# One core of Trainium2: the order in which a gathered expert layer opens its last stage

## The chip, the core and the metric

The kernel runs on one core of a Trainium2 chip. Its time is the device time of one execution in microseconds (us). Three runs of the kernel before gave 1788.18 us in the median (1787.76 to 1791.38).

## What is computed

Two transformer blocks follow each other on 256 tokens of width 1024, all in float32. Only the end of the second block is touched by the change. It is a layer of retrieved experts:

```python
q = (xn @ wq).reshape(bsz, s, PEER_HEADS, 2, PEER_HALF)          # 8 heads, 2 halves of 128
sub = einsum('bshpd,hpnd->bshpn', q, subkeys)                     # against 128 subkeys each
s_top, i_top = top_k(sub, 16)
cand = s_top[..., 0, :, None] + s_top[..., 1, None, :]            # 16 x 16 candidates
best, pos = top_k(cand, 16)                                       # 16 experts per head
gate = softmax(best)
a = gelu(einsum('td,ted->te', xn, u_tab[expert]))                 # 128 experts per token
h = h + einsum('te,ted->td', gate * a, v_tab[expert])
```

For each token and each of its 8 x 16 = 128 chosen experts one row of `u_tab` and one of `v_tab` (1024 numbers each) are fetched. The kernel stores both tables side by side as `puv`, so that one row is 8 KB.

## The kernel before

The program has one instruction stream for each engine, written by hand; semaphores count the results. Weights of all matrix products come as 128 x 1024 tiles through a `ring` of 8 slots. A tile is split into two parts so that three matmuls per product give float32 accuracy: ScalarE writes the high part (L767), VectorE the low part (L1044), both up to three tiles ahead of TensorE (`AHEAD = 3`, four slots for split tiles), and TensorE runs 24 matmuls on it (L494 to L496). ScalarE then evicts the result (L774).

The last stage is driven by one list, `PEER`, that `peer_order` writes (L206). Each engine walks the same list and carries out its own share of each step, strictly in this order:

- `queries hd`: the two query tiles of a head (tiles 2hd and 2hd+1; 16 in all). ScalarE and VectorE split tiles up to three ahead, TensorE multiplies, ScalarE evicts.
- `route t hd p`: the choice of experts for 128 tokens (block t) and one head, in five parts. Part 0: TensorE's product with the subkeys (L726), evicted by ScalarE. Parts 1 to 3: VectorE's sorting (from L1597, from L1609, from L1626). Part 3 ends with the indices in `idx`, and with an exponential on ScalarE (L1007). Part 4: VectorE's division (L1648).
- `turn_h`: TensorE turns the normalized tokens to the layout that the dot products need (L736), ScalarE evicts four banks.
- `gather t k`: GpSimd starts two indirect DMAs (L1737), one for choice k and one for k+1. A gather brings one row for each of the 128 tokens, 128 x 8 KB = 1.05 MB. There are 256.
- `dot t k`: VectorE multiplies each of the two gathered halves with the tokens and sums (L1665).
- `second t k`: ScalarE applies the gelu (L1019), the gate (L1023), and builds a diagonal matrix for each (L1029). TensorE multiplies it with the other half of the gathered rows and adds up in PSUM: two halves of 512 columns, each recorded as two matmuls, so 4 records for one gather and 8 for a pair (L749).
- `finish t`: once the 128 rows of a block are done, VectorE adds the result (L1674), and SyncE stores it.

A gather needs a free buffer. There are 17. Seven of them are early (`NE`): pieces of activation buffers that nobody reads once the tokens are normalized and turned. Ten are late: the weight `ring`, the slots of the split tiles, and the place of the operands of the query product. They come free when the last query tile has been multiplied:

```python
if before:
    q.wait_ge(*mm.at("row", *before))
elif n >= NE:
    q.wait_ge(s_lo, NW)
    q.wait_ge(*mm.at("wq", 15))
else:
    q.wait_ge(*dv.at("peer", "h", 7))
    q.wait_ge(*mm.at("turn_h", 1, 1))
```

`before` is the gather whose rows the buffer held, so it waits for TensorE's `second` on it. The seventh early buffer takes one gather only; the other 16 go round.

The list of the kernel before is: head 0's queries and its whole choice; the turning; the queries of heads 1 to 7, with the choice of head 1 between them; then 128 pairs (c = 0 to 127). A pair is gather, dot, one part of a later choice, second, as long as parts are left: 14 choices of five parts, so pairs 0 to 69. Below, "pair c" is this unit.

Of the kernel before, what the change touches and what calls it, by code (L numbers as in the profile page):

```python
# [204 lines left out]

def peer_order(early, late):  # L206

    out = [("queries", 0)] + [("route", 0, 0, p) for p in range(5)] + [("turn_h", t, h) for t in range(2) for h in range(2)]
    for hd in range(1, 8):
        out.append(("queries", hd))  # L210
        if hd >= 3:
            out.append(("route", 0, 1, hd - 3))
    work = [("route", t, hd, p) for t in range(2) for hd in range(8) for p in range(5)][10:]
    routed, buf, use = {(0, 0), (0, 1)}, {}, {}

    def more():
        if work:
            out.append(work.pop(0))
            if out[-1][3] == 3:
                routed.add(out[-1][1:3])  # L220

    free = list(range(early + late))
    for g in range(256):
        t, k = divmod(g, 128)
        n = free.pop(0)
        if n != early - 1:
            free.append(n)
        times, before = use.get(n, (0, None))
        buf[t, k] = n, times + 1, before
        use[n] = times + 1, (t, k)  # L230

    for c in range(128):
        t, k0 = divmod(2 * c, 128)
        while (t, k0 // 16) not in routed:
            more()
        out.append(("gather", t, k0))
        out.append(("dot", t, k0))
        if c == 40:
            out.extend([("turn_y", i // 2, i % 2) for i in range(4)])
        more()  # L240
        out.append(("second", t, k0))
        if k0 == 126:
            out.append(("finish", t))
    return out, buf


def program(nc, T, out, dbg=None):
    ctx = ExitStack()
    with ctx:
# [156 lines left out]
        NB = len(gbuf)  # L406
        s_g = [sem(f"row_in{i}") for i in range(NB)]
        PEER, GB = peer_order(NE, NB - NE)


# [1520 lines left out]
```

## Time and profile before

| what | value |
|---|---|
| median of the runs | 1788.18 us |
| the profiled execution | 1791.73 us, span of its instructions 1789.2 us |
| PE, DVE, ACT, POOL busy in the span | 85%, 64%, 34%, 21% |
| granted TensorE clock, mean | 0.926 |
| bytes read from HBM | 430.29 MB, of which the gathers are 268 MB |
| last stage | from about 1068 us to the end |
| chain that ended last | PE 57%, DVE 23%, DMA 12%, ACT 6% |

The profile is of one execution, and its times count from the span's first instruction. PE is TensorE, DVE VectorE, ACT ScalarE, POOL GpSimd. A row of a timeline gives start, length, engine, line, operation, what is written and read, and in brackets how long the engine had been idle and what ended that. Consecutive instructions of one kind are merged as "x8".

### The profile page before, as it was taken

To read this page: it belongs to the slowest core of one execution; us is meant where nothing else is said; L and a number is where in the kernel's file an instruction comes from. 1 tells how busy PE (TensorE), PEld (TensorE's weight loads), DVE (VectorE), ACT (ScalarE), POOL (GpSimd) and SP (SyncE) were. 2 spreads that over 40 slices of the span, in tenths; PEclk is the share of its full clock that TensorE was granted. 3 is DMA by queue.
4 is the path that set the end of the run, shared out by engine and by line. 5 is a ranking of instruction groups with operands and counts; after the bars stand their busy time and mean duration, and the time that the engine had idled before them with its cause. 6 is when DMAs were issued, how large, how long until landed. Compare 5 with 4: busy or idle time off the path is not lost.

```text
span 1789.2 us, 19560 instructions
## 1 busy us (share of the span) xinstructions
PE 1517.9 (85%) x7194; PEld 1108.8 (62%) x7194; DVE 1144.5 (64%) x2246; ACT 611.0 (34%) x1336; POOL 370.3 (21%) x376
## 2 busy tenths in 40 slices
PE   7899999997887799997988677878778777977776
PEld 6788888886764799997977577533333333432222
DVE  6876765556474665556577655887686777544444
ACT  2322222224244444443453244433333333322222
POOL 2000110010000000010000111444344343743430
PEclk8899999997989799997998888989889897999999
DMA  9554774443220255553331355699999998999997
GB/s 379 186 167 136 232 247 162 136 148 116 84 83 23 95 187 181 175 174 106 116 113 51 100 186 224 240 421 421 421 421 402 394 386 337 417 421 421 421 421 321
DMA packets 86189, 432.60 MB, mean 242 GB/s; under 512 B 9616, under 2 KB 13200, under 8 KB 53072
## 3 DMA queue, kind: packets, MB, share of 16 engines
q0 software_dynamic: 45024, 298.08, 41.9%
q1 hardware_dynamic: 41072, 133.30, 22.8%
q8 instruction: 57, 0.93, 0.2%
q14 instruction: 36, 0.29, 0.0%
HBM read 430.29 MB, written 1.05 MB: 241 GB/s over the span
## 4 chain that ended last, share of the span: by engine, by line
PE 57%; DVE 23%; DMA 12%; ACT 6%; issue 2%; POOL 0%; SPq 0%; DVEq 0%; POOLq 0%; ACTq 0%
PE ps L494 14%; PE ps L495 14%; PE ps L496 14%; DMA HF<-in_puv,AB 11%; PE ps L749 11%; DVE WR L1044 2%; DVE work L1102 2%; ACT WR L767 2%; DVE HF L1665 1%; ACT L1019 1%; DVE ring L1665 1%; DMA ring<-in_w_adaT 1%; DVE WF L1665 1%; PE ps L607 1%; DVE HR L1122 1%
## 5 line engine op out<-in xcount | busy, mean ns | idle before, releaser
L494 PE MATMUL ps<-HR,WR 128*128 128x256 f32 (+1 forms) x1336 | 438.6, 328 | 49.5 <-DVE HR L1122 15.4
L1044 DVE TENSOR_TENSOR WR<-ring,WR 128x1024 fp32r<-128x1024 f32 (+2 forms) x245 | 281.9, 1153 | 240.7 <-ACT WR L767 240.4
L495 PE MATMUL ps<-HR,WR 128*128 128x256 f32 (+1 forms) x1336 | 427.9, 320 | 0.0
L496 PE MATMUL ps<-HR,WR 128*128 128x256 f32 (+1 forms) x1336 | 427.1, 320 | 0.0
L767 ACT CAST WR<-ring 128x1024 fp32r<-128x1024 f32 (+2 forms) x245 | 237.2, 972 | 347.7 <-PE ps L496 347.6
L494 PEld LDWEIGHTS ps<-HR,WR 128*128 128x128 f32 x1336 | 265.0, 198 | 74.9 <-issue 39.4
L495 PEld LDWEIGHTS ps<-HR,WR 128*128 128x128 f32 x1336 | 266.2, 199 | 16.0 <-issue 1.2
L496 PEld LDWEIGHTS ps<-HR,WR 128*128 128x128 f32 x1336 | 265.6, 199 | 14.4
L749 PE MATMUL ps<-HF,AB 128*128 128x512 f32 x252 | 130.3, 652 | 41.6 <-ACT AB L1029 41.6
L749 PE MATMUL ps<-ring,AB 128*128 128x512 f32 x256 | 126.8, 639 | 38.8 <-ACT AB L1029 38.8
L749 PE MATMUL ps<-WF,AB 128*128 128x512 f32 x256 | 125.6, 635 | 34.7 <-ACT AB L1029 34.7
L494 PE MATMUL ps<-AR,WR 128*128 128x256 f32 (+1 forms) x416 | 137.5, 330 | 4.8 <-POOL AR L1719 4.8
L495 PE MATMUL ps<-AR,WR 128*128 128x256 f32 (+1 forms) x416 | 137.2, 330 | 0.0
L496 PE MATMUL ps<-AR,WR 128*128 128x256 f32 (+1 forms) x416 | 137.2, 330 | 0.0
L749 PEld LDWEIGHTS ps<-HF,AB 128*128 128x128 f32 x252 | 50.6, 207 | 112.5 <-ACT AB L1029 56.0
L749 PEld LDWEIGHTS ps<-ring,AB 128*128 128x128 f32 x256 | 50.4, 203 | 109.2 <-issue 54.4
L749 PEld LDWEIGHTS ps<-WF,AB 128*128 128x128 f32 x256 | 50.3, 202 | 105.5 <-issue 55.3
L1019 ACT ACTIVATE AB<-AB 128x2 f32<-128x2 f32 x128 | 25.7, 201 | 239.6 <-DVE AB L1665 239.4
L1665 DVE CUSTOM_DVE_ANT_0 WF<-WF,AF 128x1024 f32<-128x1024 f32 x64 | 77.3, 1220 | 38.1 <-DMA WF<-in_puv,AB 38.1
L1665 DVE CUSTOM_DVE_ANT_0 ring<-ring,AF 128x1024 f32<-128x1024 f32 x64 | 77.1, 1220 | 32.7 <-DMA ring<-in_puv,AB 32.7
L1665 DVE CUSTOM_DVE_ANT_0 HF<-HF,AF 128x1024 f32<-128x1024 f32 x63 | 76.5, 1221 | 31.9 <-DMA HF<-in_puv,AB 31.8
L1694 POOL DMA_DIRECT2D AB<-in_w_adaT x56 | 29.8, 532 | 323.7 <-DVE Mr L1055 282.2
(244 smaller groups left out, 2270.7 us busy)
## 6 DMA issues: line engine op xcount, KB each, us to landing
AB<-in_w_adaT POOLq DMA_DIRECT2D x56, 512.0 KB, 4.7
ring<-in_f1i SPq DMA_DIRECT2D x44, 512.0 KB, 4.5
ring<-in_f2i SPq DMA_DIRECT2D x44, 512.0 KB, 3.5
ring<-in_w SPq DMA_DIRECT2D x33, 512.0 KB, 3.6
ring<-in_mi SPq DMA_DIRECT2D x19, 512.0 KB, 3.5
ring<-in_f1o SPq DMA_DIRECT2D x16, 512.0 KB, 4.2
ring<-in_f2o SPq DMA_DIRECT2D x16, 512.0 KB, 3.5
ring<-in_wq SPq DMA_DIRECT2D x16, 512.0 KB, 4.3
```

The lines of the kernel that those rows point to most:

```text
L494: e.matmul(o, l[0], r[0], start=first, stop=False)
L495: e.matmul(o, l[0], r[1], start=False, stop=False)
L496: return e.matmul(o, l[1], r[0], start=False, stop=last)
L607: x = e.matmul(o[o_:o_ + 64, 0:256], vN[:, k, 64 * kv:64 * kv + 64], PT[:, hd % 2, k, :], start=k == 0, stop=k == 3)
L749: x = e.matmul(psum[ab + h][:, :], D[:, nd % 8, :], gbuf[n][:, 1024 + 512 * h:1536 + 512 * h], start=k == 0, stop=k == 127)
L767: e.copy(WS[:, m % NSP, 0, 0:nk * cols], ring[:, (NA + m) % NS, 0:nk * cols]).then_inc(s_hi, 1)
L1019: e.activation(w_, w_, ACT.Gelu_apprx_tanh).then_inc(*ac.to("gelu", t_, k0))
L1044: e.tensor_tensor(WS[:, m % NSP, 1, 0:nk * cols], ring[:, (NA + m) % NS, 0:nk * cols], WS[:, m % NSP, 0, 0:nk * cols].bitcast(F32), ALU.su ...
L1102: e.reciprocal(r, r).then_inc(*dv.to("recip", *key))
L1122: e.scalar_tensor_tensor(out=low, in0=F[:, f, a], scalar=sh[:, s:s + 1], in1=hi.bitcast(F32), op0=ALU.add, op1=ALU.subtract).then_inc(*dv. ...
L1665: e.tensor_tensor_reduce(u_, u_, hN[:, t_, :], 1.0, 0.0, ALU.mult, ALU.add, av[:, t_, k:k + 1]).then_inc(*dv.to("dot", t_, k))
L1694: e.dma_start(AB[:, 3072 + 1024 * s_:4096 + 1024 * s_], T["w_adaT"][i]).then_inc(s_a[s_], 16)
```

## The change

Only `peer_order` changes. The whole difference:

```diff
-    out = [("queries", 0)] + [("route", 0, 0, p) for p in range(5)] + [("turn_h", t, h) for t in range(2) for h in range(2)]
-    for hd in range(1, 8):
-        out.append(("queries", hd))
-        if hd >= 3:
-            out.append(("route", 0, 1, hd - 3))
-    work = [("route", t, hd, p) for t in range(2) for hd in range(8) for p in range(5)][10:]
-    routed, buf, use = {(0, 0), (0, 1)}, {}, {}
+    out = [("queries", 0), ("route", 0, 0, 0)] + [("turn_h", t, h) for t in range(2) for h in range(2)]
+    out += [("route", 0, 0, 1), ("route", 0, 0, 2), ("queries", 1), ("route", 0, 0, 3), ("route", 0, 0, 4), ("queries", 2)]
+    work = [("route", t, hd, p) for t in range(2) for hd in range(8) for p in range(5)][5:]
+    routed, buf, use = {(0, 0)}, {}, {}
...
-    free = list(range(early + late))
+    free = list(range(early))
     for g in range(256):
+        if g == 13:
+            free = list(range(early, early + late)) + free
...
         out.append(("dot", t, k0))
+        if c < 5:
+            out.append(("queries", c + 3))
         if c == 40:
```

The new list is: head 0's queries, the first part of its choice, the turning, the rest of the choice with head 1's queries between its parts, head 2's queries. Then the pairs begin. The queries of heads 3 to 7 stand inside pairs 0 to 4, after the dot products and before the second product. The choice of head 1 fills pairs 0 to 4 too, and every later choice stands five pairs later than before, so parts are left for pairs 0 to 74. Gathers 7 to 12 use six early buffers a second time; gather 13 is the first that takes a late buffer.

The operations and their number stay the same. On ScalarE, the eviction of the turned tokens (`AF<-ps` of 512 columns) moves ahead of the exponential. Before:

```order
L774 COPY AF<-ps2 128x256
L1007 ACT_TABLE_LOAD
L1007 ACTIVATE AB,small<-AF,small 128x16
L774 COPY AF<-ps3 128x512
L774 COPY AF<-ps0 128x512
L774 COPY AF<-ps1 128x512
L774 COPY AF<-ps2 128x512
L767 CAST WR<-ring 128x1024
L774 COPY AB<-ps3 128x256
L767 CAST WR<-ring 128x1024
```

and now (all lines below L206 stand one line lower):

```order
L775 COPY AF<-ps3 128x512
L775 COPY AF<-ps0 128x512
L775 COPY AF<-ps1 128x512
L775 COPY AF<-ps2 128x512
L768 CAST WR<-ring 128x1024
L775 COPY AB<-ps3 128x256
L768 CAST WR<-ring 128x1024
L775 COPY AB<-ps0 128x256
L1008 ACT_TABLE_LOAD
L1008 ACTIVATE AB,small<-AF,small 128x16
L768 CAST WR<-ring 128x1024
L775 COPY AB<-ps1 128x256
```

The four evictions come first now, then a split tile and a query's eviction, twice, and only then the exponential.

The place where head 1's exponential and the first gelus stand, also ScalarE. Before, from the query evictions on:

```order
L774 COPY AB<-ps2 128x256
L774 COPY AB<-ps3 128x256
L1007 ACTIVATE AB,small<-AF,small 128x16
L774 COPY AB<-ps0 128x256
L774 COPY AB<-ps1 128x256
L774 COPY AF<-ps2 128x256
L1019 ACT_TABLE_LOAD
L1019 ACTIVATE AB<-AB 128x2
L1023 ACTIVATE AB<-AB 128x1 x2
```

and now, in pairs 3 and 4:

```order
L768 CAST WR<-ring 128x1024
L775 COPY AB<-ps2 128x256
L775 COPY AB<-ps3 128x256
L1008 ACT_TABLE_LOAD
L1008 ACTIVATE AB,small<-AF,small 128x16
L1020 ACT_TABLE_LOAD
L1020 ACTIVATE AB<-AB 128x2
L1024 ACTIVATE AB<-AB 128x1 x2
L1030 ACTIVATE AB<-kc,AB 128x128 x2
L775 COPY AB<-ps0 128x256
L775 COPY AB<-ps1 128x256
```

The exponential stands between the evictions of tiles 12 and 13 and those of tiles 14 and 15 as before, but now a table load is ahead of it and another behind it, and the first product of pair 3's rows comes ahead of tiles 14 and 15.

GpSimd's gathers with what they wait for. Before:

```order
L1737 DMA AF<-in_puv,AB 128x2048 [waits pe_group,dve_result]
L1737 DMA AF<-in_puv,AB 128x2048
L1737 DMA HF<-in_puv,AB 128x2048 x2
L1737 DMA work<-in_puv,AB 128x2048 x2
L1737 DMA AF<-in_puv,AB 128x2048
L1737 DMA ring<-in_puv,AB 128x2048 [waits pe_group,low_part]
L1737 DMA ring<-in_puv,AB 128x2048 x3
```

and now:

```order
L1738 DMA AF<-in_puv,AB 128x2048 [waits pe_group,dve_result]
L1738 DMA AF<-in_puv,AB 128x2048
L1738 DMA HF<-in_puv,AB 128x2048 x2
L1738 DMA work<-in_puv,AB 128x2048 x2
L1738 DMA AF<-in_puv,AB 128x2048
L1738 DMA AF<-in_puv,AB 128x2048 [waits pe_group] x2
L1738 DMA HF<-in_puv,AB 128x2048 [waits pe_group] x2
L1738 DMA work<-in_puv,AB 128x2048 [waits pe_group] x2
L1738 DMA ring<-in_puv,AB 128x2048 [waits pe_group,low_part]
```

After the first seven, the next ones wait for TensorE's second product on the gather whose buffer they take, where before the eighth waited for the last query tile; that wait now stands at the fourteenth.

## Rows read from the trace of the kernel before

**Rows 1.** Busy time by stretch; last columns: granted clock, DMA share, GB/s
```profile
core 0: us, PE busy (x) PEld busy (x) DVE busy (x) ACT busy (x) POOL busy (x), PEclk, DMA share, GB/s
1200.00:1300.00 100.00, 76.88 (x161) 33.67 (x162) 72.36 (x204) 34.92 (x114) 40.77 (x35) 0.86 1.01 421
1470.00:1520.00 50.00, 33.99 (x63) 14.21 (x62) 36.84 (x92) 17.95 (x61) 17.52 (x15) 0.80 0.90 348
1555.00:1785.00 230.00, 175.46 (x383) 68.84 (x381) 112.08 (x182) 59.05 (x230) 82.60 (x81) 1.00 0.98 407
```
**Rows 2.** Timeline of PE, the stage's opening: start, length, what [idle before]
```profile
1090.14 0.58 PE L494 MATMUL ps<-HR,WR 128*128 128x256 f32 x1 [8.95 <-ACT AF L774]
...
1133.48 0.61 PE L726 MATMUL ps<-XT,AB 128*128 128x128 f32 x4
...
1136.88 5.33 PE L749 MATMUL ps<-AF,AB 128*128 128x512 f32 x8 [2.79 <-ACT AB L1029]
...
1142.05 3.60 PE L749 MATMUL ps<-HF,AB 128*128 128x512 f32 x8
```
**Rows 3.** Timeline of ACT, the same stretch
```profile
1089.22 0.31 ACT L1007 ACTIVATE AB<-AF,small 128x16 f32<-128x16 f32 x1 [8.06 <-DVE small L1644]
...
1089.52 2.02 ACT L774 COPY AF<-ps 128x512 f32<-128x512 f32 x4
...
1095.67 0.37 ACT L774 COPY AB<-ps 128x256 f32<-128x256 f32 x1 [3.18 <-PE ps L496]
...
1133.68 0.37 ACT L774 COPY AB<-ps 128x256 f32<-128x256 f32 x1 [2.51 <-PE ps L496]
...
1135.81 0.20 ACT L1019 ACTIVATE AB<-AB 128x2 f32<-128x2 f32 x1
...
1148.17 0.31 ACT L1007 ACTIVATE AB<-AF,small 128x16 f32<-128x16 f32 x1 [5.49 <-DVE small L1644]
...
1148.59 1.28 ACT L1019 ACT_TABLE_LOAD   x1
...
1149.89 0.20 ACT L1019 ACTIVATE AB<-AB 128x2 f32<-128x2 f32 x1
```
**Rows 4.** Timeline of DVE, the same stretch
```profile
1079.88 0.29 DVE L1597 MAX8 AF<-AF 128x8 f32<-128x128 f32 x1 [1.66 <-ACT AF L774]
...
1083.16 0.42 DVE L1609 TENSOR_TENSOR AF<-AF 128x256 f32<-128x256 f32 x1
...
1086.27 0.18 DVE L1626 CAST AF<-AF 128x32 f32<-128x32 uint32 x1
...
1124.76 1.22 DVE L1044 TENSOR_TENSOR WR<-ring,WR 128x1024 fp32r<-128x1024 f32 x1
...
1129.61 1.22 DVE L1665 CUSTOM_DVE_ANT_0 AF<-AF 128x1024 f32<-128x1024 f32 x1
...
1158.97 0.29 DVE L1597 MAX8 AF<-AF 128x8 f32<-128x128 f32 x1 [0.90 <-ACT AF L774]
```
**Rows 5.** Timeline of POOL: the first and the eighth gather
```profile
1089.40 1.00 POOL L1737 DMA_INDIRECT AF<-in_puv,AB  x1 [26.88 <-DVE small L1644]
...
1134.42 0.94 POOL L1737 DMA_INDIRECT ring<-in_puv,AB  x1 [35.37 <-PE ps L726]
```
**Rows 6.** The gathers' table, seen by its own view
```profile
DMA to landing us min/median/max: 5.3/21.1/34.0
```
**Rows 7.** Timeline of PE over the repeating part
```profile
1157.92 0.61 PE L726 MATMUL ps<-XT,AB 128*128 128x128 f32 x4
...
1175.42 3.78 PE L749 MATMUL ps<-HF,AB 128*128 128x512 f32 x4 [4.95 <-ACT AB L1029]
...
1185.23 0.61 PE L726 MATMUL ps<-XT,AB 128*128 128x128 f32 x4
...
1458.45 0.61 PE L726 MATMUL ps<-XT,AB 128*128 128x128 f32 x4
...
1492.96 0.61 PE L726 MATMUL ps<-XT,AB 128*128 128x128 f32 x4
```
**Rows 8.** The chain that ended last, in order of time
```profile
1510.46 44.05 PE ps L749 x96
```

## The prediction

> **What bounds the kernel now.** I read the busy time by stretch first, then the timelines of the last stage's opening engine by engine, then the chain of waits. All stages up to 1068 us keep their instructions, so only the last one counts.
>
> By stretch [rows 1], the DMA engines are full from 1200 to 1300 us at 421 GB/s. A gather is 128 x 8 KB = 1.05 MB, so it takes 1.05 / 0.421 = 2.49 us, and a pair 4.98. Between 1470 and 1520 us the share falls to 0.90 and 348 GB/s, at the end it is 0.98. So DMA is nearly the bound, but something else holds it back in the middle. The repeating part shows what. The subkey product opens each choice of experts, once in five pairs. It stands at 1157.92 us, then at 1185.23, and eleven choices after the first at 1458.45 [rows 7]: (1458.45 - 1157.92) / 11 = 27.3 us for five pairs, where DMA needs 24.9. TensorE is idle for 4.95 us in each, waiting for the diagonals behind the choice, and then takes 3.78 us for four records [rows 7], against 3.60 for eight elsewhere [rows 2]: that is the clock at 1.2 and not 2.4 GHz. So **the five-pair loop is slower than DMA by 2.4 us**, and after enough loops the 16 buffers are used up and the loop sets when gathers start. When the last choice is over, TensorE runs 96 records, 24 gathers' rows, in 44.05 us without a pause [rows 8]. That is 1.84 us a row against 2.49, so it catches up with DMA, and DMA alone sets the end.
>
> The end is therefore: start of the loops, plus their number times 27.3, plus what DMA still has to bring. The opening counts by when the loop at pair 5 begins, and in two places by when gathers land.
>
> **The opening of before.** TensorE has turned the tokens by 1081.2 us, then stands for 8.95 us until 1090.14 [rows 2], because ScalarE evicts the turned tokens only at 1089.52, behind the exponential of 1089.22 [rows 3]. The next tile runs at the lower clock, 1090.14 to its eviction at 1095.67. From there 13 tiles and a subkey product take 1133.68 - 1095.67 = 38.0 us, 2.88 a tile. The last query tile is done at 1133.48 [rows 2], and GpSimd starts gather 7 at 1134.42 [rows 5]; 0.95 us later.
>
> **The change, step by step.**
>
> *The turning.* The four evictions no longer wait for the choice. TensorE begins head 1 at 1081.2, at the clock that it has. The saving at the first tile is 1095.4 - (1081.2 + 2.88) = 11.3 us.
>
> *The first gather.* Two split tiles (1.15 us each by their spacing, 1.22 in the row [rows 4]) now stand on VectorE between parts 2 and 3. Part 3 began at 1086.27 [rows 4], and now begins at 1088.6. The first gather starts at 1089.40 + 2.3 = 1091.7 [rows 5]. The shortest time to landing is 5.3 us [rows 6], so it lands by 1097.0, the second no sooner than 1099.5, and its dot product (1.22) ends at 1100.7.
>
> *TensorE, heads 1 and 2 and 3.* Six tiles, 17.3 us, to 1098.5, and 0.6 for the subkey product. Then it waits for the first diagonal: from the gelu to the product takes 1136.88 - 1135.81 = 1.07 us [rows 2, 3], so it starts at 1101.8. That is an idle time of 2.7 us, and after 2.79 us before, the first eight records took 5.33 and not 3.60 [rows 2]. I take 5.33: pair 0 ends at 1107.1.
>
> *Pairs 1 and 2.* Two tiles, 5.76. Then the second product waits for ScalarE, which evicts the second tile first: 0.3 us to its start, 0.27 for it, 1.07 from gelu to product, 1.6 together. Then 3.45 for eight records. 10.8 a pair, to 1128.7. VectorE has in each pair two split tiles, two dot products (1.15 each [rows 4]) and one part of a choice (1079.88 to 1083.16 is 3.3, the next 3.1 [rows 4]), 8 us in all, and hides in TensorE's time. The gathers of these pairs are the first seven and land by about 1115.
>
> *Pair 3.* 5.76 to 1134.5, then 0.57 for the eviction, a table load of 1.28, the exponential 0.42 (1148.17 to 1148.59), a load of 1.30 (1148.59 to 1149.89) [rows 3] and 1.07: product at 1139.1, 4.6 us idle, 5.33 for it, to 1144.4. These two loads are new on the path. I charge 1.3 us for each, what the row shows with everything around it. The Trainium skill ("ScalarE: Activation LUTs", What ACT_TABLE_LOAD costs) says that a switch takes about 2.66 us, since 1.38 us of drain come on top of the load. By the page the two would cost 2.8 us more, and the sum below would be +3.9 and not +1.1.
>
> *Pair 4 and the late buffers.* Two tiles to 1150.2. **The last query tile is 16.7 us later than before**, because four pairs of second products (3.45 to 5.33 each) and the waits around them now stand ahead of it. Gather 13 starts at 1151.1 and lands at 1156.4. Before, it was the seventh behind 1134.42: 1139.7 + 6 x 2.49 = 1154.7. So six gathers early and a late wait nearly cancel, and gather 13 is 1.7 us later than before. The early ones, 7 to 12, take buffers whose rows are done by 1128.7, and land before 1136; they hide.
>
> *Pair 5.* Pair 4's second product ends at 1150.2 + 1.6 + 3.45 = 1155.3, and the subkey product follows, 2.6 us before 1157.92. VectorE must first do pair 6's dot products, the second of them on gather 13, until 1157.6. It begins sorting there and not at 1158.97 [rows 4]. **The loops begin 1.3 us earlier**, and at the same pair c = 5.
>
> *One loop more.* Parts of a choice last for pairs up to 74, not 69. The five pairs 70 to 74 take 27.3 and not DMA's 24.9: +2.4 us. The stop between the two blocks of tokens (1458.45 to 1492.96 is 34.5 and not 27.3 us [rows 7]) lies at pair 64 in both, in the same part of a loop, and costs the same.
>
> *Sum.* -1.3 + 2.4 = **+1.1 us** on the profiled execution's 1791.73. The median of the runs lies 3.5 us below that; I add the change to the median, 1788.18 + 1.1 = **1789.3**. Not shown by the trace is whether a start 1.3 us earlier survives 14 loops, each with its fall of the clock. An earlier product does more of its work at the lower clock, so all of it may be lost (0). Or the fall ends sooner in a loop, which saves at most what the slow four records lose, 3.78 - 1.80 = 2.0 us; allowing that twice beside the 1.3 gives -5.3 for the loops. With the +2.4 the bounds are -2.9 and +2.4.
>
> A measurement of this kernel can tell about 0.2%, 3.6 us, from no change.
>
> **Rivals.**
>
> *Faster, the opening runs without waits.* If ScalarE is never behind and the clock stays up, TensorE's work alone is 1081.2 + 14 x 2.88 + 4 x 3.45 = 1135.3: the late gathers start only 2 us later than before, with 13 done. Pair 5 begins at about 1140, 18 us earlier. Gather 13 lands at 1141.6, 13 us before 1154.7, so DMA then is the limit: -13, about 1775. For it speaks that 24 rows run without a pause [rows 8]; against it that ScalarE's order puts an eviction ahead of every gelu, and in pair 3 the two loads. A part of it would be enough to pass 3.6 us. Chance 0.14.
>
> *Slower, the clock falls in every opening pair.* TensorE stops for 1.6 us in each of the pairs 1, 2 and 4. If each stop brings the lower clock, the product behind it takes 5.33 and not 3.60: 3 x 1.7 = 5.2 us. Sorting at pair 5 then begins 3.9 us later than before, and the late gathers, behind pairs 1 and 2, 3.5 us later still. The end is +1.1 + 5.2 = +6.3, 1794.5. It decides from 2.5 us of added delay in the opening. For it speaks how close 2.79 us of idle time comes, against it that the tiles around the stops are dense work. Chance 0.16.
>
> *Slower, a switch of tables costs more than its row.* The two new loads stand ahead of pair 3's product with nothing beside them, so what a switch costs beyond 1.3 us goes to the end twice. It decides from 1.25 us more in each: +1.1 + 2.5. Against it speaks that between the end of the exponential and the gelu lie 1.30 us, and the load fills 1.28 of them [rows 3]; nothing is left for more. With the cost of one such load paid again each time, the end is 1.1 + 2.6 = +3.7, about 1792. Chance 0.04. This is the case that the Trainium skill's figure, above, would make.
>
> *The early gathers do nothing.* If DMA alone set the end, then only the start of gather 13 would count, +1.7 us. That is inside the forecast's band.
>
> **How the numbers follow.** The forecast with its bounds, and the last rival, stay within 3.6 us: 0.66. Faster 0.14, slower 0.16 + 0.04 = 0.20. For 8 in 10 the range has to reach past the bounds -2.9 to +2.4 to about half of each rival: 1783 to 1795.
>
> **What would show it.** Right: no 9-us gap of TensorE after the turning, first gather about 2.3 us later, the last query tile at 1150 with GpSimd's gather 13 one us behind it, the subkey product of pair 5 at about 1155, the following ones 27.3 apart, and one more of them at the end. Idle times of TensorE of about 2.7, 1.6, 1.6, 4.6 and 1.6 us in pairs 0 to 4. Wrong: a last query tile before 1145 or after 1154 us, loops other than 27.3 us, or a DMA share between 1470 and 1520 us that reaches 1.0.

## The result, and the profile after

The changed kernel took 1797.88 us in the median of six runs (1792.85 to 1798.67). The kernel before, in six runs, took 1788.78 us (1787.23 to 1791.89). The ratio is 1.0044, 95% interval 1.0032 to 1.0057: the change made the kernel slower by 0.3 to 0.6%. The forecast was 1789.3 us, no measurable change, and a range up to 1795. It was wrong.

The profiled executions are 1797.77 us against 1791.73, and their spans 1795.8 and 1789.2, so 6.0 to 6.6 us can be followed in the two traces. The interval of the ratio is 5.7 to 10.2 us, and they lie inside it. In both the last stage begins at the same place: head 0's subkey product starts at 1078.42 us now, and at 1078.33 before.

The timeline of TensorE (PE) in the opening, which answers to [rows 2] and [rows 7]. All names below stand one line lower than before.

```profile
1098.39 0.61 PE L727 MATMUL ps<-XT,AB 128*128 128x128 f32 x4
...
1105.64 5.62 PE L750 MATMUL ps<-AF,AB 128*128 128x512 f32 x8 [6.64 <-ACT AB L1030]
...
1118.37 3.70 PE L750 MATMUL ps<-HF,AB 128*128 128x512 f32 x8 [1.37 <-ACT AB L1030]
...
1129.19 3.70 PE L750 MATMUL ps<-work,AB 128*128 128x512 f32 x8 [1.37 <-ACT AB L1030]
...
1143.14 5.40 PE L750 MATMUL ps<-AF,AB 128*128 128x512 f32 x8 [4.50 <-ACT AB L1030]
...
1155.65 1.98 PE L750 MATMUL ps<-AF,AB 128*128 128x512 f32 x4 [1.37 <-ACT AB L1030]
...
1159.19 0.61 PE L727 MATMUL ps<-XT,AB 128*128 128x128 f32 x4
...
1188.54 0.61 PE L727 MATMUL ps<-XT,AB 128*128 128x128 f32 x4
```

The 8.95 us gap at head 1 [rows 2] is gone. In its place TensorE stops five times: 6.64, 1.37, 1.37, 4.50 and 1.37 us ahead of the products of pairs 0 to 4. The first product took 5.62 us for eight records and the fourth 5.40; those in between took 3.70. Pair 5's subkey product is at 1159.19 and not at 1157.92, and pair 10's at 1188.54 and not at 1185.23: 1.3 us late, then 3.3 us late.

POOL, the first two gathers and the fourteenth (before [rows 5]), then VectorE (DVE) with what it waited for:

```profile
1091.64 1.01 POOL L1738 DMA_INDIRECT AF<-in_puv,AB  x1 [29.01 <-DVE small L1645]
...
1092.95 1.94 POOL L1738 DMA_INDIRECT AF<-in_puv,AB  x1 [0.30 <-issue]
...
1155.06 0.94 POOL L1738 DMA_INDIRECT ring<-in_puv,AB  x1 [20.28 <-PE ps L497]
```

```profile
1092.83 2.44 DVE L1045 TENSOR_TENSOR WR<-ring,WR 128x1024 fp32r<-128x1024 f32 x2 [0.51 <-ACT WR L768]
...
1097.37 1.22 DVE L1666 CUSTOM_DVE_ANT_0 AF<-AF 128x1024 f32<-128x1024 f32 x1 [2.10 <-DMA AF<-in_puv,AB]
...
1103.31 1.23 DVE L1666 CUSTOM_DVE_ANT_0 AF<-AF 128x1024 f32<-128x1024 f32 x1 [4.70 <-DMA AF<-in_puv,AB]
...
1160.59 1.23 DVE L1666 CUSTOM_DVE_ANT_0 ring<-ring,AF 128x1024 f32<-128x1024 f32 x1 [15.94 <-DMA ring<-in_puv,AB]
```

The last query tile was done at 1154.1 us, 0.95 us ahead of gather 13, where before it was 1133.48. Gather 1 was used only at 1103.31, 11.7 us after gather 0 was started.

ScalarE (ACT) in pair 3:

```profile
1139.07 1.28 ACT L1008 ACT_TABLE_LOAD   x1
...
1140.36 0.31 ACT L1008 ACTIVATE AB<-AF,small 128x16 f32<-128x16 f32 x1
...
1140.78 1.28 ACT L1020 ACT_TABLE_LOAD   x1
...
1142.07 0.20 ACT L1020 ACTIVATE AB<-AB 128x2 f32<-128x2 f32 x1
```

A load, the exponential, a load, the gelu: 3.0 us, the loads at 1.28 us and their start.

The busy time by stretch, where the last two columns are the share of the DMA engines and GB/s:

```profile
core 0: us, PE busy (x) PEld busy (x) DVE busy (x) ACT busy (x) POOL busy (x), PEclk, DMA share, GB/s
1116.00:1140.00 24.00, 19.90 (x121) 15.47 (x119) 19.50 (x51) 7.94 (x19) 5.62 (x4) 1.00 0.60 223
1140.00:1155.00 15.00, 11.14 (x56) 7.92 (x56) 3.82 (x8) 4.32 (x13) 0.00 (x0) 0.89 0.00 0
1155.00:1160.00 5.00, 4.14 (x12) 2.04 (x12) 0.00 (x0) 1.06 (x5) 3.74 (x4) 1.00 0.68 223
```

For 15 us, from 1140 to 1155, the DMA engines moved nothing at all. Thirteen gathers had come, and the fourteenth waited for a late buffer.

The end of the repeating part, PE, and the piece of the chain of waits behind it (before [rows 7, 8]):

```profile
1461.96 0.61 PE L727 MATMUL ps<-XT,AB 128*128 128x128 f32 x4
...
1496.44 0.61 PE L727 MATMUL ps<-XT,AB 128*128 128x128 f32 x4
...
1523.48 0.61 PE L727 MATMUL ps<-XT,AB 128*128 128x128 f32 x4
```

```profile
1540.98 54.48 PE ps L750 x120
```

The stop between the blocks is 34.5 us as before. One loop more stands behind it, 27.0 us. The run of products without a pause that catches up with DMA begins at 1540.98 and not at 1510.46, and takes 120 records and not 96.

### The profile page after: what moved, and what is told of

Same layout as the page of the kernel before. It is cut to its first block, busy times and chain, and to the rows that moved or that the text cites. A ratio compares the mean times of both kernels' runs of the same rounds, so it can differ in the third digit from the quotient of the medians.

```text
span 1795.8 us, 19544 instructions
## 1 busy us (share of the span) xinstructions
PE 1521.2 (85%) x7194; PEld 1109.4 (62%) x7194; DVE 1144.0 (64%) x2246; ACT 612.7 (34%) x1338; POOL 373.3 (21%) x376
## 4 chain that ended last, share of the span: by engine, by line
PE 57%; DVE 22%; DMA 11%; ACT 6%; issue 2%; POOL 1%; SPq 0%; DVEq 0%; POOLq 0%; ACTq 0%
PE ps L495 14%; PE ps L496 14%; PE ps L497 14%; PE ps L750 12%; DMA ring<-in_puv,AB 10%; DVE WR L1045 2%; DVE work L1103 2%; ACT WR L768 2%; DVE ring L1666 1%; ACT L1020 1%; DVE WF L1666 1%; DVE HF L1666 1%; DMA ring<-in_w_adaT 1%; PE ps L608 1%; DVE HR L1123 1%
## 5 line engine op out<-in xcount | busy, mean ns | idle before, releaser
L750 PE MATMUL ps<-WF,AB 128*128 128x512 f32 x240 | 121.8, 652 | 37.4 <-ACT AB L1030 37.4
L750 PE MATMUL ps<-AF,AB 128*128 128x512 f32 x140 | 73.2, 659 | 31.5 <-ACT AB L1030 31.5
```

The lines of the kernel that those rows point to most:

```text
L750: x = e.matmul(psum[ab + h][:, :], D[:, nd % 8, :], gbuf[n][:, 1024 + 512 * h:1536 + 512 * h], start=k == 0, stop=k == 127)
```

## The experiments

Two theories stood at first. **Theory A:** the turning ahead of the choice is worth what the opening saves. The interleaving (the queries of heads 3 to 7 inside the pairs) then loses more, since four pairs' products, their waits and a loop more stand ahead of or behind the last query tile. **Theory B:** DMA and the clock set the time, so the opening matters little, and early gathers are worth their transfer. All kernels compute the whole reference. The short diffs are against the kernel named; lines of `peer_order` that only carry the bookkeeping along are left out.

The traces are compared by stage, since the place of the stage's start moved between profiles (last section). "Pair 5" and "pair 10" are the starts of these pairs' subkey products behind the stage's first one; "stage" is the span's end less the stage's first subkey product; "rest" is stage less pair 10. All are from the profiled executions, in us. The loops are those that start at pair 5 or later. Each ratio is against executions of before taken together with the kernel's; their medians were 1788.92 us for e1 to e4, 1789.11 for e5 to e7 and 1787.99 for e8 and e9.

| kernel | median | ratio, 95% | pair 5 | pair 10 | loops | rest | stage |
|---|---|---|---|---|---|---|---|
| before | 1788.78 | | 79.6 | 106.9 | 13 | 604.0 | 710.9 |
| the change | 1797.88 | 1.0044 (1.0032 to 1.0057) | 80.8 | 110.1 | 14 | 607.3 | 717.4 |
| e1, turning alone | 1779.05 | 0.9946 (0.9928 to 0.9963) | 71.8 | 97.8 | 13 | 602.6 | 700.4 |
| e2, no interleaving | 1774.48 | 0.9920 (0.9904 to 0.9936) | 67.9 | 94.1 | 13 | 603.0 | 697.1 |
| e3, one loop more | 1793.21 | 1.0020 (1.0010 to 1.0030) | 79.2 | 106.7 | 14 | 607.6 | 714.3 |
| e4, first gather | 1796.85 | 1.0041 (1.0028 to 1.0055) | 80.5 | 108.2 | 14 | 605.6 | 713.8 |
| e5, two heads inside | 1784.03 | 0.9978 (0.9967 to 0.9989) | 76.9 | 104.1 | 13 | 603.2 | 707.3 |
| e6, one loop less | 1780.66 | 0.9960 (0.9947 to 0.9973) | 77.5 | 104.1 | 12 | 599.6 | 703.7 |
| e7, diagonals first | 1785.30 | 0.9976 (0.9966 to 0.9985) | 69.4 | 100.3 | 14 | 607.3 | 707.6 |
| e8, no first stop | 1783.68 | 0.9976 (0.9967 to 0.9985) | 70.1 | 100.0 | 14 | 607.2 | 707.2 |
| e9, e7 and e8 | 1790.77 | 1.0007 (0.9997 to 1.0017) | 72.5 | 103.8 | 14 | 607.8 | 711.6 |

The column "rest" carries the reading of them all. It is 602.6 to 604.0 with 13 loops, 599.6 with 12, and 607.2 to 607.8 with 14 (605.6 in e4). What happens ahead of pair 10 reaches the end in full, within 1.4 us in all kernels but e4, and a loop costs about 3.5 us. How many gathers are early does not show in it: the change, with thirteen, has 607.3, and e3, with seven and as many loops, 607.6.

### e1: the turning alone

```diff
-    out = [("queries", 0)] + [("route", 0, 0, p) for p in range(5)] + [("turn_h", t, h) for t in range(2) for h in range(2)]
+    out = [("queries", 0), ("route", 0, 0, 0)] + [("turn_h", t, h) for t in range(2) for h in range(2)] + [("route", 0, 0, p) for p in range(1, 5)]
```

> The kernel before, with the turning of the tokens alone moved ahead of parts 1 to 4 of the first choice; all queries stay ahead of the pairs and the buffers stay as before. Theory A (the opening's gain is real, and the interleaved queries lose it again): TensorE goes on after 1081 us for three tiles, waits for the next split tile, and has the last query tile about 8 us before 1133.5; the loops follow, so the end is 6 to 9 us below before. Theory B (DMA and clock decide, the opening does not matter): within 2 us of before.

Measured: 1779.05 us, 9.9 below before in the medians, the stage 10.5 us shorter. Theory A's mechanism held, and its 6 to 9 us were a little low. This part of the change alone is a gain of half a per cent.

### e2: no interleaving

Against before; the two lines after `out` are those of the change.

```diff
-    out = [("queries", 0)] + [("route", 0, 0, p) for p in range(5)] + [("turn_h", t, h) for t in range(2) for h in range(2)]
-    for hd in range(1, 8):
+    out = [("queries", 0), ("route", 0, 0, 0)] + [("turn_h", t, h) for t in range(2) for h in range(2)]
+    out += [("route", 0, 0, 1), ("route", 0, 0, 2), ("queries", 1), ("route", 0, 0, 3), ("route", 0, 0, 4), ("queries", 2)]
+    for hd in range(3, 8):
         out.append(("queries", hd))
-        if hd >= 3:
-            out.append(("route", 0, 1, hd - 3))
+        out.append(("route", 0, 1, hd - 3))
```

> The change's opening up to head 2's queries, but heads 3 to 7 and head 1's choice stay ahead of the pairs, and the late buffers follow the first seven as before. Theory A: last query tile at about 1122 us instead of 1154, gather 7 then, loops 10 to 12 us earlier than before and none more than before: end about 10 us below before. If six gathers more in the early buffers were worth what they bring (15 us), this kernel would lose against the change; theory A has it 18 us ahead of the change.

Measured: 1774.48 us, 14.4 us below before and 23.4 below the change, the fastest kernel of this study; theory A had expected 10 and 18. PE, then POOL's eighth gather; the stage began at 1074.32 here:

```profile
1121.16 5.40 PE L749 MATMUL ps<-AF,AB 128*128 128x512 f32 x8 [2.79 <-ACT AB L1029]
...
1142.22 0.61 PE L726 MATMUL ps<-XT,AB 128*128 128x128 f32 x4
...
1168.39 0.61 PE L726 MATMUL ps<-XT,AB 128*128 128x128 f32 x4
```

```profile
1118.71 0.94 POOL L1737 DMA_INDIRECT ring<-in_puv,AB  x1 [20.38 <-PE ps L726]
```

The last query tile was done 0.95 us ahead of 1118.71, 43.4 us into the stage, against 75.7 in the change (1154.1 - 1078.4). Six gathers fewer were early, and DMA moved nothing between 1112 and 1120 us. Even so, the change, with 13 early gathers, is the slower one by 20.3 us of stage. So the end does not follow DMA's early start. What the six early gathers are worth by themselves this run does not tell, since it changes the place of the queries with them.

### e3: one loop more

Against before: head 1's choice is left out of the opening, and the choices start in pair 0 with head 1.

```diff
         out.append(("queries", hd))
-        if hd >= 3:
-            out.append(("route", 0, 1, hd - 3))
-    work = [("route", t, hd, p) for t in range(2) for hd in range(8) for p in range(5)][10:]
+    work = [("route", t, hd, p) for t in range(2) for hd in range(8) for p in range(5)][5:]
```

> The kernel before with one thing of the change: head 1's choice is made inside pairs 0 to 4, every later one five pairs later, so parts last to pair 74. Last query tile unchanged at 1133.5 us. The loop takes 27.3 us where DMA takes 24.9, so theory A expects +2.4 us, at most +6 if the loops start at another phase of the clock. Rival: the DMA queue absorbs it, 0.

Measured: 1793.21 us, +4.3 in the medians (+1.8 to +5.4 by the interval), +3.4 in the stage. Pairs 5 and 10 stay in place within 0.4 us; the whole of it lies in the rest. So DMA does not absorb a loop, and its price is 3.4 us where I had 2.4.

### e4: the first gather earlier

Against the change:

```diff
-    out += [("route", 0, 0, 1), ("route", 0, 0, 2), ("queries", 1), ("route", 0, 0, 3), ("route", 0, 0, 4), ("queries", 2)]
+    out += [("route", 0, 0, 1), ("route", 0, 0, 2), ("route", 0, 0, 3), ("queries", 1), ("route", 0, 0, 4), ("queries", 2)]
```

> The change, with head 1's queries behind part 3 of the first choice instead of between parts 2 and 3, so the first index is out 2.3 us earlier and the next split tiles 2.9 us later. If the 6.6 us stop of TensorE ahead of pair 0's product (and the slow clock behind it) is what the late first gather costs, pair 0's product starts 2 us earlier and the end is 2 to 4 us below the change; if the landing beside the weight tiles sets it, no difference from the change.

Measured: 1796.85 us, the same as the change within the intervals. In the profile the stage is 3.6 us shorter, but that execution is not a typical one of its kernel (1793.45 us against a median of 1796.85). Pair 0's product:

```profile
1103.76 5.40 PE L750 MATMUL ps<-AF,AB 128*128 128x512 f32 x8 [2.79 <-ACT AB L1030]
```

From the stage's start (1076.53) that is 27.2 us, which is the change's 27.2 (1105.64 - 1078.42) exactly. The first gather went out 2.1 us earlier, but TensorE was behind: head 2's second tile waits for a split tile that now comes later. The stop is shorter by 3.9 us and the product at the same place. The experiment moved the wait and did not take it away, and so does not tell what the late landing costs; e8 takes the long stop away, though not by itself.

### e5: two heads inside

Against e2: heads 3 to 5 stay ahead with all of head 1's choice, heads 6 and 7 go into pairs 0 and 1.

```diff
-    for hd in range(3, 8):
+    for hd in range(3, 6):
         out.append(("queries", hd))
         out.append(("route", 0, 1, hd - 3))
+    out += [("route", 0, 1, 3), ("route", 0, 1, 4)]
...
         out.append(("dot", t, k0))
+        if c < 2:
+            out.append(("queries", c + 6))
```

> Run e2 with the queries of heads 6 and 7 alone inside pairs 0 and 1; head 1's choice stays ahead, loops as many as before, seven early gathers. Theory A (what stands ahead of the last query tile is what counts): the last tile waits for the first gather's landing at about 1103 us and for one pair of rows, so it comes at about 1120 to 1128 (counted with the stage's start at 1078), and the end lies 2 to 10 us above e2. Rival (interleaving costs only by the extra loop and not by the place of the last tile): same as e2 within 2 us.

Measured: 1784.03 us, 9.6 above e2. The stage is 10.2 us longer, pair 10 is 10.0 us later, the rest is equal. So interleaving costs without any loop more, as theory A has it; the rival is out. The last query tile comes 54.7 us into the stage, some 5 us later than theory A had put it.

### e6: one loop less

Against e2:

```diff
+    rr = [("route", 0, h, p) for h in (1, 2) for p in range(5)]
     for hd in range(3, 8):
         out.append(("queries", hd))
-        out.append(("route", 0, 1, hd - 3))
+        out += [rr.pop(0), rr.pop(0)]
```

> Run e2 with head 2's choice ahead of the pairs as well, two parts behind each of heads 3 to 7. One loop less (13), the last query tile unchanged; but VectorE has 10 us more to do before the first dot product, so pair 0 starts about 6 us later. If a loop is worth what e3 showed (3.4 us in the profiles) and the later start is hidden by DMA: 3 us below e2. If the loops' start counts fully: 3 us above e2 or more.

Measured: 1780.66 us, 6.2 above e2. The rest is shorter by 3.4 us, which gives the price of a loop from the other side. But pair 10 comes 10.0 us later, and this start counts in full, as the expectation's second case had it. That VectorE's whole further choice ahead of the first dot product makes it late is the reason given beforehand; no run separates it.

### e7: diagonals first

Against the change, in ScalarE's program alone. It walks a list in which, for pairs 0 to 4, the queries and the part of the choice stand behind the second product's share.

```diff
+            mine, held = [], []
             for s in PEER:
+                if s[0] == "queries" and s[1] >= 3 or held and s[0] == "route":
+                    held.append(s)
+                elif s[0] == "second":
+                    mine += [s] + held
+                    held = []
+                else:
+                    mine.append(s)
+            for s in mine:
```

> The change, with ScalarE alone in another order in pairs 0 to 4: gelu and diagonals come ahead of the two query evictions and of the exponential. The stops of TensorE ahead of the products of pairs 1 to 4 (1.37, 1.37, 4.50, 1.37 us, and the slow clock in pair 3) should go. If they are what the interleaving costs, the last query tile comes 8 to 10 us earlier than in the change and the end lies 7 to 10 us below it. If the second products themselves (four pairs ahead of the last tile, 14 us at full clock) and the first landing are the larger part, it still does not reach run e2: about 1788 against 1774.

Measured: 1785.30 us, 12.6 below the change where 7 to 10 were expected, the stage 9.8 us shorter. PE, the products of pairs 0 to 3:

```profile
1103.16 5.61 PE L750 MATMUL ps<-AF,AB 128*128 128x512 f32 x8 [6.61 <-ACT AB L1039]
...
1114.35 3.60 PE L750 MATMUL ps<-HF,AB 128*128 128x512 f32 x8
...
1123.53 3.60 PE L750 MATMUL ps<-work,AB 128*128 128x512 f32 x8
...
1132.72 3.60 PE L750 MATMUL ps<-AF,AB 128*128 128x512 f32 x8
```

The three later ones start without a stop and at full speed; the first stop of 6.6 us is still there. Pair 5 comes 11.4 us earlier than in the change, pair 10 9.8 us: 1.6 us are lost again in the first loop, 30.9 us long, since gather 13, which pair 6's dot products need, had started only 2.5 us ahead of pair 5's subkey product (1142.85 and 1145.34).

### e8: no first stop

Against the change:

```diff
-    ... ("route", 0, 0, 4), ("queries", 2)]
+    ... ("route", 0, 0, 4), ("queries", 2), ("queries", 3)]
...
-        if c < 5:
-            out.append(("queries", c + 3))
+        if c in (0, 1, 2, 4):
+            out.append(("queries", c + 4 - c // 4))
```

> The change, with head 3's queries ahead of pair 0 and those of heads 4, 5, 6 and 7 inside pairs 0, 1, 2 and 4. As many second products (four pairs) stand ahead of the last query tile as in the change, the same thirteen gathers are early, the same loops follow; but TensorE has two more tiles to do while the first two gathers land. Theory: the stop of 6.64 us ahead of pair 0's product, with the slow clock behind it (5.62 for 3.70 us, and part of the next tile), is the term that was priced too low. Then the last query tile comes 6 to 9 us earlier than the change's 1154 us and the end lies 6 to 9 us below the change, about 1790. Rival (the clock or the landing of gather 13 sets the loops, whatever the first stop): within 2 us of the change.

Measured: 1783.68 us, 14.2 below the change where 6 to 9 were expected, the stage 10.2 us shorter. PE, pairs 0 to 3, with the stage's start at 1074.19:

```profile
1103.32 3.70 PE L750 MATMUL ps<-AF,AB 128*128 128x512 f32 x8 [2.79 <-ACT AB L1030]
...
1114.13 3.70 PE L750 MATMUL ps<-HF,AB 128*128 128x512 f32 x8 [1.37 <-ACT AB L1030]
...
1124.95 3.70 PE L750 MATMUL ps<-work,AB 128*128 128x512 f32 x8 [1.37 <-ACT AB L1030]
...
1129.98 3.70 PE L750 MATMUL ps<-AF,AB 128*128 128x512 f32 x8 [1.32 <-ACT AB L1030]
```

Pair 0's product stops for 2.79 us and takes 3.70 and not 5.62. Pair 3's product follows pair 2's after 1.32 us, where in the change two tiles, the exponential and a fall of the clock lay between. The number of products ahead of the last query tile, the early gathers and the loops are the change's. So of the change's 717.4 us some 10 are stops of TensorE that another order of the same steps avoids. The edit took away more than the first stop, the one of pair 3 too, so it does not split the 10 us between them.

### e9: both

Against the change: the edits of e7 and e8, with `s[1] >= 4` in e7's condition.

> Run e8 with ScalarE's order of run e7 (diagonals ahead of the query evictions and the exponential). If the first stop and the later stops are separate costs, they add: about 15 to 19 us below the change, and of the 23 us between the change and run e2 only the loop more (3.4) and the products ahead of the last tile are left: 1779 to 1783. If DMA's late start takes over (gather 13 lands behind the loops), it stays within 3 us of e7's 1785.

Measured: 1790.77 us, 7.1 above e8 alone, 5.5 above e7, and above both ranges that had been expected (1779 to 1783, or within 3 us of e7). What the two edits save does not add. PE's product of pair 3, and ScalarE ahead of it:

```profile
1136.31 5.76 PE L750 MATMUL ps<-AF,AB 128*128 128x512 f32 x8 [8.48 <-ACT AB L1039]
```

```profile
1133.54 0.31 ACT L1017 ACTIVATE AB<-AF,small 128x16 f32<-128x16 f32 x1 [7.43 <-DVE small L1654]
```

With the diagonals first, ScalarE is early in pair 2 and then stands for 7.43 us at head 1's exponential, which waits for VectorE; the diagonals of pair 3 are behind it. In pair 3 there is no query tile for TensorE to do in that time, so it stops for 8.48 us. The wait that the edit removed came back elsewhere.

## Why the prediction was wrong, by its own steps

- **What bounds the kernel: right.** Loops 27.3 us apart, each dearer than DMA's ten rows; then a run without pause, then DMA. The table's "rest" shows it in all eleven kernels. That gathers' landings count too held for gather 13, which VectorE waited for at pair 6, and for no later one that the table would show.
- **The turning: right in kind.** TensorE went on at once. Pair 0's subkey product came at 1098.39, predicted 1098.5. By e1 this part alone is worth 10 us.
- **The first gather: the step that failed.** I took the second gather's landing at its earliest, 2.49 us behind the shortest landing, 1099.5. Its dot product started at 1103.31, 3.8 us later. A lower bound had been put in as the value. The trace of before already had a better one. Its DMA issues, from issue to landing in us: gathers 0 and 1 of before (issued at 1089.40 and 1090.71), then gather 1 of e7 (at 1090.50) and the weight tile issued behind it (at 1091.63):

```profile
AF<-in_puv,AB POOLq DMA_INDIRECT x1, 5.3
...
AF<-in_puv,AB POOLq DMA_INDIRECT x1, 8.0
...
AF<-in_puv,AB POOLq DMA_INDIRECT x1, 10.3
...
ring<-in_wq SPq DMA_DIRECT2D x1, 512.0 KB, 8.9
```

  In before the second gather landed 4.0 us behind the first, not 2.49: that is 1.5 of the 3.8 us. Another 1.0 is the longer issuing (last section). The weight tile could be the rest: in e7 it landed 0.3 us ahead of gather 1, and its bytes are half a gather's, 1.25 us by 2.49. No run left the tile out, so this last part is not shown.

  The product of pair 0 started at 1105.64 and not at 1101.8, a stop of 6.64 us and not 2.7. Everything behind it in the opening is later by just this: the last query tile 1154.1 and not 1150.2, pair 5 1159.2 and not 1155.3.
- **Pairs 1, 2 and 4: right.** Stops of 1.37 us where I had 1.6, products of 3.70 where I had 3.45.
- **Pair 3 and the table loads: right.** 4.50 us where I had 4.6, 5.40 where I had 5.33. The loads took 1.28 us. By that, the 2.66 us for a switch that the Trainium skill ("ScalarE: Activation LUTs", What ACT_TABLE_LOAD costs) states is not paid here: from the load's start at 1140.78 to the gelu at 1142.07 lie 1.29 us.
- **The loops' start: wrong by 4.6 us.** Sorting at pair 5 was to begin 1.3 us earlier than before. It stands behind the dot product of 1160.59, 1.2 us long, so it began 2.8 us later than 1158.97. 3.9 of these 4.1 us are the first landing; the landing of gather 13 itself, 5.5 us after its start, was 0.2 longer than the 5.3 in the sum. Another 0.5 us came in the first loop: pair 10 is 3.3 us late.
- **One loop more: right in kind, too small.** +2.4 was predicted; e3 has +3.4 (and in its medians +4.3), e6 -3.4 for one less. I had set the loop against ten rows at 421 GB/s. In the change DMA moved 354 GB/s from 1496.44 to 1523.48 us, the loop behind the stop between the blocks, and 421 from 1600 to 1780, which leaves about 4.3 of these 27.0 us unused by DMA where I had 2.4. How this comes to the 3.4 of the whole stage the traces do not split.
- **The sum.** With the measured terms, +3.3 at pair 10 and +3.3 in the rest (607.3 - 604.0) make 6.6 us, and the spans differ by 6.6 (1795.8 - 1789.2).
- **The base.** The profiled execution of before lay 3 us above its median, that of the change at its median. The medians differ by 9.1 us, of which the traces show 6. The other 3 need no cause of their own: the traces' 6.0 to 6.6 lie inside the interval, and at the profile's granted clock of 0.925 or 0.926 nine executions of before took 1790.94 to 1792.07 us and three of the change 1797.77 to 1798.67, 6.6 apart in their medians.
- **The rivals.** The clock rival gave 1794.5, near the profile's +6, but not by its mechanism: behind the stops of 1.37 us the products took 3.70 us, full speed. The faster rival asked what this order would bring without waits, 1775. Not reached: e7 and e8, which take away part of the stops, land at 1785.3 and 1783.7, and e2's 1774.5 comes from not interleaving. The rival of the dearer table switch is answered by the 1.29 us above. The last rival, DMA alone by the start of gather 13, is out by e6: there gather 13 starts 1.1 us later in the stage than in e2 (53.8 and 52.7), and pair 10 comes 10.0 us later. For this rival I had put gather 13's landing in before at 1154.7; its trace has 1156.8 (issued at 1142.74, 14.1 us to landing), mostly by the same second gather taken at 2.49.

So the change has a part that gains about 10 us (e1), or 14 us together with head 1's queries between the parts of the choice (e2), and a part that loses 23 us in the medians, 20.3 in the stage (the change against e2). In the stage the losing part is made of the loop more, 3.4 to 4.3 us, and of pair 10's later start, 16.0 us (110.1 - 94.1). About 10 of these 16 are stops and slow records, which e7 or e8 each take away. For the 6 that are left the products of four pairs ahead of the last query tile are the likely cause; no run tests it alone. The thirteen early gathers bring nothing that any run shows, but that was not tried by itself, since with seven early buffers the interleaved order would wait for itself.

## What to carry to other kernels

A resource that is busy most of the time need not be the one whose head start counts: here bringing six transfers forward came with a loss of 20.3 us in the stage against e2, since a loop of dependent steps on four engines set the end, and each of its turns had to be started as early as possible. Before work is interleaved, ask what it stands in front of. Four short products ahead of the last tile also put four handovers between engines ahead of it. In a sum, a shortest time seen is a bound; the first two uses of a queue that has been at rest are to be priced from two such uses in the trace, 5.3 us and 4.0 behind it here.

## What the runs showed of the hardware

- **Starting gathers from rest.** In the change and in e1, e2 and e4 to e9, whose VectorE split a tile at that moment, GpSimd's second gather took 1.94 or 1.95 us to issue; in the kernel before and in e3, whose VectorE was then at rest or in short instructions, 0.97. The Trainium skill ("GPSIMD Engine Reference", 1. Specifications) says that GpSimd shares its SBUF interfaces with VectorE, with contention for instructions that have two SBUF inputs; the splitting is one, and the rows agree. It explains one of the four us by which the second landing was late.
- **The second landing from rest.** In before, gather 1 landed 4.0 us behind gather 0, and gather 8, issued when no weight tile was on its way any more, 4.2 us behind gather 7 (5.4 and 8.4 us to landing, issued at 1134.42 and 1135.66). The next one followed after 2.5.
- **Two stops, two speeds behind them.** After 1.37 us of idle time eight records took 3.70 us; after 4.50 and 6.64 us they took 5.40 and 5.62. After 2.79 us it was 5.33 before [rows 2], 5.40 in e2 and e4, but 3.70 in e8; the granted clock over these records was 0.69 in before, 0.68 in e2 and e4, and 1.00 in e8. The same length of stop does not always bring the lower clock.
- **The stage's start moves.** Its first product began between 1074.2 us (e8) and 1078.8 us (e3) after the span's start, though every instruction ahead of it is the same in all eleven kernels. That is more than the 0.2% of a measurement, and the reason why the stages are compared here by their own length. It goes with the execution's mean granted clock: 1078.3 to 1078.8 us at 0.925 or 0.926 (before, the change, e3, e9), 1074.2 to 1075.1 at 0.928 to 0.931 (e2, e5, e6, e8), 1075.9 to 1076.5 at 0.934 to 0.937 (e1, e4, e7).
